# A hybrid decoder step on one core: the first tile's norm in column halves, and its gain spread by GpSimd

## The reference

```python
def layer(x, p, ...):
    mix, pool_buf, v = mixer(rmsnorm(x, norm_mix), ...)   # the first norm; its gain is norm_mix
    x = x + mix
    x = x + moe(rmsnorm(x, norm_ffn), ...)                # top 4 of 32 experts, clamped SwiGLU
    x = x + sigmoid(x @ w_ple_gate) * (p @ w_ple_proj)
    return x, pool_buf, v

def rmsnorm(x, g):
    y = x * lax.rsqrt(jnp.mean(x * x, axis=-1, keepdims=True) + RMS_EPS)
    return y * g

def mixer(h, ...):
    z = h @ w_in          # columns: pooling part z, then u and v of the gating part
    ...                   # pooling mixer and gating mixer, concatenated, @ w_out
```

## Time and profile before

| | us |
|---|---|
| median of 3 runs | 1396.92 |
| lowest and highest | 1396.46, 1397.35 |
| the profiled execution, own time | 1394.86 |
| its span, first to last instruction | 1393.1 |
| PE busy | 1358.1 (97% of the span) |
| DVE busy | 1264.1 (91%) |
| ACT busy | 936.1 (67%) |
| POOL busy | 237.9 (17%) |

### The profile page before, as it was taken

How to read it: one execution, slowest core, us unless ns; L and a number is a source line. 1 busy time by engine, 2 the same in 40 slices (tenths; PEclk the granted TensorE clock), 3 DMA queues, 4 the chain that set the end, 5 groups by cost and what they waited for, 6 DMA issues and landing times.

```text
span 1393.1 us, 19627 instructions
## 1 busy us (share of the span) xinstructions
PE 1358.1 (97%) x6479; PEld 1122.8 (81%) x6479; DVE 1264.1 (91%) x1003; ACT 936.1 (67%) x635; POOL 237.9 (17%) x190
## 2 busy tenths in 40 slices
PE   6999989999999999999999999999999999999997
PEld 5998767888888888888888888888888888888565
DVE  5876578999999999999999999999999999999885
ACT  4313256777777777777777777777777777777532
POOL 3130021112111111111111111111111111110100
PEclk9999979999999999999999999999999999999999
DMA  7112377999999999999999999999999999999551
GB/s 269 61 64 104 143 291 285 383 357 372 391 388 380 385 381 384 381 379 377 379 383 382 379 379 382 381 381 388 384 382 379 384 386 384 380 385 367 192 231 62
DMA packets 94204, 457.09 MB, mean 328 GB/s; under 512 B 13347, under 2 KB 14927, under 8 KB 60310
## 3 DMA queue, kind: packets, MB, share of 16 engines
q1 hardware_dynamic: 84383, 437.77, 80.8%
q0 software_dynamic: 9360, 17.85, 3.3%
q10 hardware_dynamic: 430, 1.08, 0.3%
HBM read 451.50 MB, written 21.58 MB: 340 GB/s over the span
## 4 chain that ended last, share of the span: by engine, by line
PE 95%; DVE 2%; issue 1%; ACT 1%; DMA 1%; POOL 0%; POOLq 0%; DVEq 0%; ACTq 0%
PE ps L1454 50%; PE ps L1463 25%; PE ps L1293 4%; PE ps L1433 2%; PE ps L1440 2%; PE ps L1606 2%; PE ps L1394 1%; PE ps L1202 1%; PE ps L1204 1%; PE ps L1209 1%; PE ps L1149 1%; PE ps L1326 1%; DVE resid L2144 1%; PE ps L1143 1%; PE ps L1146 1%
## 5 line engine op out<-in xcount | busy, mean ns | idle before, releaser
L1923 DVE TENSOR_TENSOR w_lo<-raw,w_hi 128x2048 fp32r<-128x2048 f32 x384 | 870.4, 2298 | 21.5 <-PE ps L1463 21.1
L978 ACT ACTIVATE w_hi<-raw 128x2048 fp32r<-128x2048 f32 x384 | 732.8, 1917 | 229.6 <-PE ps L1454 142.8
L1454 PE MATMUL ps<-w_hi,xT_hi 128*128 128x512 f32 x1024 | 280.0, 395 | 4.5 <-ACT w_hi L978 3.4
L1454 PE MATMUL ps<-w_hi,xT_lo 128*128 128x512 f32 x1024 | 275.8, 391 | 0.0
L1463 PE MATMUL ps<-w_lo,xT_hi 128*128 128x512 f32 x1024 | 274.0, 389 | 0.0
L1454 PEld LDWEIGHTS ps<-w_hi,xT_lo 128*128 128x128 f32 x1024 | 193.6, 189 | 41.1
L1454 PEld LDWEIGHTS ps<-w_hi,xT_hi 128*128 128x128 f32 x1024 | 190.9, 189 | 43.9 <-issue 3.4
L1463 PEld LDWEIGHTS ps<-w_lo,xT_hi 128*128 128x128 f32 x1024 | 192.1, 188 | 40.2 <-DVE w_lo L1923 0.2
L803 POOL PARTITION_BROADCAST up_bias<-bias_rows x32 | 41.5, 1296 | 655.4 <-DVE glu L2003 649.2
L1454 PE MATMUL ps<-w_hi,aT_hi 128*128 128x512 f32 x512 | 140.1, 395 | 0.6 <-ACT aT_hi L997 0.6
L1454 PE MATMUL ps<-w_hi,aT_lo 128*128 128x512 f32 x512 | 137.2, 390 | 0.1
(11 more groups left out here) (297 smaller groups left out, 1218.0 us busy)
## 6 DMA issues: line engine op xcount, KB each, us to landing
raw<-in_w_up_dram SPq DMA_DIRECT2D x256, 1024.0 KB, 7.6
raw<-in_w_down_dram SPq DMA_DIRECT2D x128, 1024.0 KB, 8.0
raw<-in_w_ple_gate_dram SPq DMA_DIRECT2D x4, 1024.0 KB, 4.9
yk<-expert_rows SPq DMA_DIRECT2D x4, 1024.0 KB, 7.7
raw<-expert_rows SPq DMA_DIRECT2D x4, 1024.0 KB, 6.5
resid<-in_x_prompt_dram SPq DMA_DIRECT2D x4, 512.0 KB, 7.7
w_v_sb<-in_w_in_dram SPq DMA_DIRECT2D x2, 1024.0 KB, 8.1
w_z_sb<-in_w_in_dram SPq DMA_DIRECT2D x2, 1024.0 KB, 13.0
```

Of the source, the lines that this page charges most:

```text
L978: act.activation(w_hi[:, s % SPLIT, :], raw[:, slot(s), :], ACT.Copy).then_inc(s_hi, 1)
L1454: mm = pe.matmul(out[:, c:c + 512], (xh, xl)[xs], w_hi[:, s % SPLIT, base + c:base + c + 512], start=(fresh and xs == 0 and base == 0), st ...
L1923: dve.tensor_tensor(w_lo[:, s % SPLIT, :], raw[:, slot(s), :], w_hi[:, s % SPLIT, :].bitcast(F32), ALU.subtract).then_inc(s_lo, 1)
```

## The change

The 4 KB row of `norm_mix` is loaded alone, into the first partition of `x_rows` (a tile that is free until the expert loop), and POOL spreads it over the partitions of `gain` with `partition_broadcast`, after the identity and ahead of the first root. DVE waits for that instead of for the load. For tile 0, the product with root and gain, the transposes, the high part and the low part are each cut in two halves of 512 columns (four blocks), and DVE makes `w_v_low(0)` between the two low halves. `project_v(0, 0)` needs the first halves alone. The counts on `s_job`, `s_xn`, `s_xh` and `s_emptied["V"]` go up by one accordingly. Tiles 1 to 4 are done as before.

```diff
-            EMPTIED[name] = sum(w == who for _, w in JOBS[:n + 1])
+            EMPTIED[name] = sum(w == who for _, w in JOBS[:n + 1]) + (who == "V")
...
             pool.affine_select(out=ident[:], in_=ident[:], compare_op=ALU.not_equal, fill=1.0, base=0,
                                pattern=[[-1, P]], channel_multiplier=1).then_inc(s_ident, 1)
+            pool.wait_ge(ld["gain"], 16)
+            pool.partition_broadcast(gain[:], x_rows[0:1, :]).then_inc(s_gain, 1)
...
-            act.dma_start(gain[:], norm_mix[0].partition_broadcast(P)).then_inc(ld["gain"], 16)
+            act.dma_start(x_rows[0:1, :], norm_mix[0:1, :]).then_inc(ld["gain"], 16)
...
             square1(0)
             w_v_high(0)
-            x_high(0)
+            for half in range(2):
+                act.wait_ge(s_job, 1 + half)
+                act.activation(xTh[:, w_z_halves[half], 0:P], bank(("xT", 0), half).rearrange("p (b n) -> p b n", n=P),
+                               ACT.Copy).then_inc(s_xh, 1)
             square1(1)
...
-                pe.wait_ge(s_xh, t + 1)
+                pe.wait_ge(s_xh, 1 if t == 0 and i == 0 else t + 2)
...
-                    pe.wait_ge(s_emptied["V"], EMPTIED[("xT", t)])
+                    pe.wait_ge(s_emptied["V"], 1 if t == 0 and i == 0 else EMPTIED[("xT", t)])
...
                 if what == "xT":
-                    pe.wait_ge(s_xn, t + 1)
+                    if t == 0:
+                        for k in range(KD):
+                            if k % (KD // 2) == 0:
+                                pe.wait_ge(s_xn, 1 + k // (KD // 2))
+                            mm = pe.transpose(bank(("xT", 0), k // 4)[:, (k % 4) * P:(k % 4 + 1) * P],
+                                              xn[:, 0, k * P:(k + 1) * P], ident[:])
+                            if k % (KD // 2) == KD // 2 - 1:
+                                mm.then_inc(s_job, 1)
+                        project_v(0, 0)
+                        continue
+                    pe.wait_ge(s_xn, t + 2)
                     transposes(("xT", t), xn[:, t % 2, :])
-                    if t == 0:
-                        project_v(0, 0)
...
-            dve.wait_ge(ld["gain"], 16)
+            dve.wait_ge(s_gain, 1)
...
-                dve.scalar_tensor_tensor(out=xn[:, t % 2, :], in0=resid[:, t, :], scalar=rstd1[:, t:t + 1], in1=gain[:],
-                                         op0=ALU.mult, op1=ALU.mult).then_inc(s_xn, 1)
+                for cols in (slice(0, D // 2), slice(D // 2, D)) if t == 0 else (slice(0, D),):
+                    dve.scalar_tensor_tensor(out=xn[:, t % 2, cols], in0=resid[:, t, cols], scalar=rstd1[:, t:t + 1],
+                                             in1=gain[:, cols], op0=ALU.mult, op1=ALU.mult).then_inc(s_xn, 1)
...
             norm1(0)
-            w_v_low(0)
-            x_low(0)
+            for half in range(2):
+                dve.wait_ge(s_xh, half + 1)
+                ks = w_z_halves[half]
+                dve.tensor_tensor(xTl[:, ks, 0:P], bank(("xT", 0), half).rearrange("p (b n) -> p b n", n=P),
+                                  xTh[:, ks, 0:P].bitcast(F32), ALU.subtract).then_inc(s_emptied["V"], 1)
+                if half == 0:
+                    w_v_low(0)
             norm1(1)
```

More of the change, by code:

```diff
@@ L365, in job_filled @@
         def job_filled(eng, name):
-            eng.wait_ge(s_job, JOB[name] + 1)
+            eng.wait_ge(s_job, JOB[name] + 2)
         ld = {n: sem("ld_" + n) for n in (
@@ L397, in build @@
         s_olow = sem("last_tile_low_rows")
+        s_gain = sem("first_norm_weights_spread")
         s_bias_hi = sem("down_bias_hi")
@@ L560, in _ @@
             sp.dma_start(new_pool_sample[0, :, 0:PB - DS, :], state_pool[0, :, DS:PB, :]).then_inc(s_pout, 16)
-            sp.wait_ge(s_job, JOB[("v", LAST)] + 1)
+            sp.wait_ge(s_job, JOB[("v", LAST)] + 2)
             for k in range(0, KD, 4):
@@ L565, in _ @@
             w_out_v = w_out.rearrange("a (i k p) n -> p (a i) k n", p=P, k=KD // 2)
-            sp.wait_ge(s_job, JOB[("z", G - 1)] + 1)
+            sp.wait_ge(s_job, JOB[("z", G - 1)] + 2)
             load(w_out_a[:], w_out_v[:, 0], "w_out")
-            sp.wait_ge(s_job, JOB[("u", G - 1)] + 1)
+            sp.wait_ge(s_job, JOB[("u", G - 1)] + 2)
             load(w_out_b[:, 0:KD // 4, :], w_out_v[:, 1, 0:KD // 4, :], "w_out2")
@@ L625, in _ @@
                     load_bias(0, 0)
-                sp.wait_ge(s_xn, TT + t + 1)
+                sp.wait_ge(s_xn, TT + t + 2)
                 sp.dma_start(xn_dram[t * P:t * P + NT[t], :], xn2[0:NT[t], :]).then_inc(s_xrow[t], 16)
@@ L754, in _ @@
                     src = dst
-            pool.wait_ge(s_job, JOB[("u", G - 1)] + 1)
+            pool.wait_ge(s_job, JOB[("u", G - 1)] + 2)
             pool.memset(x_rows[:], 0.0).then_inc(s_xzero, 1)
@@ L1669, in norm1 @@
                     job_filled(dve, ("xT", t - 2))
-                dve.scalar_tensor_tensor(out=xn[:, t % 2, :], in0=resid[:, t, :], scalar=rstd1[:, t:t + 1], in1=gain[:],
-                                         op0=ALU.mult, op1=ALU.mult).then_inc(s_xn, 1)
+                for cols in (slice(0, D // 2), slice(D // 2, D)) if t == 0 else (slice(0, D),):
+                    dve.scalar_tensor_tensor(out=xn[:, t % 2, cols], in0=resid[:, t, cols], scalar=rstd1[:, t:t + 1],
+                                             in1=gain[:, cols], op0=ALU.mult, op1=ALU.mult).then_inc(s_xn, 1)
             def x_low(t):
-                dve.wait_ge(s_xh, t + 1)
+                dve.wait_ge(s_xh, t + 2)
                 cols = slice(t * P, t * P + NT[t])
```

## The result

The changed kernel takes **1409.48 us** (median of 4 runs, 1408.77 to 1410.38), the kernel before 1396.69 us in the same comparison (median of 4, 1395.58 to 1397.35). The ratio is 1.0098, 95% interval 1.0085 to 1.011: slower by 12.8 us. The forecast was 1408.8 us. The profiled execution of the changed kernel took 1408.80 us, that of before 1394.86 us.

The account below looks back on a forecast made before the run. PE was taken to bound the kernel once it has data, after the first root. Root end 21.1 with two loads, less 8.13 before and 1.1 for halves, gives +11.9 on 1396.92: 1408.8 us, range 1401 to 1415.

Parts of the forecast that it names:

- a shift passes through: From tile 2's transposes on, PE follows PE, so a shift there was claimed to reach the end in full.
- Both pairs paid: POOL's head: configuration pairs ahead of broadcast and first root each cost a code load, 8.2 us each; chance 0.77 within bounds.
- Rival (a): POOL's head: only the first load is paid, root's code returns for nothing; +4.0, 1400.9 us; chance 0.13.
- Rival (b): POOL's head: neither pair costs visible time, halves and smaller load are won; 1394.3 us, not slower; chance 0.04.
- The price of a load: Time from a POOL configuration pair to its operation in the head: 8.2 us, between 6.13 and 10.3.
- the high bound: Dearest load price in the head, 6.13 stretched by the gathers' 7.4 / 4.4: 10.3 us, giving +16.1.
- the middle: Load price of 8.2 us taken between low and high, as gathers queue on DMA engines and no load packets were seen.
- "agree": Claim that the expert loop's 6.13 us from pair to broadcast matches the Trainium skill's 5.95 us for a first call.
- The halves: Tile 0 cut in halves, counted from the first root's end to tile 2's transposes: saves about 1.1 us (1.0 to 1.7).
- The smaller load: 512 KB less head traffic: tile 0 and w_v up to 1.5 us sooner, but nothing gained with the late root.
- The sum: First root's end at 21.1 against 8.13, less 1.1 for the halves: +11.9 us, added to the median 1396.92.
- rest of the load: Possible remainder of a load in a broadcast, from the loop's 3.39 instead of 1.30: 2.1 us more, +18.2 at the high price.

Follow-up runs that it names:

- e1_halves: Changed kernel with the first norm's weights loaded as 512 KB as before, so tile 0's halves alone: 1396.14 us against 1395.62 before, ratio 0.9999.
- e5_pe_spread: Changed kernel with the row spread by two PE matmuls and DVE copies instead of POOL's broadcast: 1394.36 us against 1395.92 before, ratio 0.9988.
- e4_no_root: Changed kernel with the first norm's roots taken off POOL, DVE making a reciprocal of the variance instead, square root left out: 1401.19 us (one run).
- e3_quiet: Changed kernel with SP issuing nothing behind tile 0 until the first root is done, keeping head traffic away: 1408.14 us (one run).
- e2_spread: Kernel before with the small load and POOL's broadcast, tile 0 done whole without halves: 1411.47 us, ratio 1.0111.
- e6_twice: Changed kernel with the broadcast of the gain done twice, no configuration pair between: 1409.29 us (one run).

## Why the prediction was right, and where it was off

**What bounds the kernel, and that a shift passes through.** Right. Tile 2's transposes moved by 13.70 us (21.98 to 35.68), and the profiled executions differ by 13.94. The first gathered rows, at +13.76, and PE's end, at +13.95, show the same shift: the kernels run in step from the head on. For small gains the assumption holds less well: in the profiled executions e1_halves keeps 0.48 of its 0.73 and e5_pe_spread about 0.9 of its 2.76 through the loop. The term that is missing is the stretch of lower clock in the router and the first expert, which need not move with the work.

**Both pairs paid.** Right, and it decided the size; the sign would have been the same with one. The trace of the changed kernel has both idle stretches; e4_no_root, which takes the root off POOL, gets about 8 us back, keeps the first and is still 5.6 over the kernel before. Rival (a), with the code back for nothing, would have had the root at 12 to 13; it started at 22.63. Rival (b) would have had it at 6 to 8. The 0.1 us at L688, which spoke for (a), was no measure of a pair that has code to bring back.

**The price of a load.** The term that was mis-sized is the first: 8.2 taken, 10.55 measured, and 9.95 to 10.33 in the other runs with the full head, so about the high bound of 10.3 or just past it. The step that failed was the choice of the middle: it held that a load might not queue with the other transfers. e3_quiet shows that this load is stretched by the head's traffic from 5.59 to 10.55. The second pair came out at 8.13 against 8.2, but not for the reason given. It was taken to be as dear as the first and stretched alike; it costs 7.3 by itself, and with the engines full 7.26, 7.35, 8.13 and 9.09 in four kernels, so the traffic's share of it lies between nothing and 1.8. By the Trainium skill's figure for both pairs the estimate had been 1404.3; the chip was 5.2 us above it. The prediction's "agree" was too quick: the Trainium skill's 5.95 ("GPSIMD Engine Reference", section 2.1 Instruction dispatch) is the gap less the wait for events, and of the 6.13 in the loop 3.08 was the wait for the gathered rows (184.0 to 187.08). Counted in that way 3.05 would be left. The near figure is the quiet head's 5.59, where the row is there early (at 2.93 in e5_pe_spread) and hardly any of the gap is wait; so the load ran during the wait, as the prediction had read it.

**The halves.** 1.1 taken off; the root's end to tile 2 went from 13.85 to 12.46, which is 1.39, and 1.53 against e2_spread. It lies in the range of 1.0 to 1.7. As foreseen, the transposes ran without a gap and DVE's order set tile 2. What the prediction didn't say is that the number holds only behind a late root. e1_halves shows it: with the root in its old place the split of w_v on ACT is later than the transposes, and the gain is 0.73 at tile 2. Rival (b) took the 1.1 in full for just that case. Its 2.6 us for halves and smaller load together is near the 2.76 that e5_pe_spread, which has both and no broadcast, shows at tile 2, but that is luck: the halves gave less there and the smaller load more.

**The smaller load.** Right that it gives nothing here. Its worth was put too low: tile 0 is squared from 4.10 instead of 5.96, 1.86 sooner, and w_v comes 2.02 sooner (7.01 against 9.03 in the trace of before), where up to 1.5 was taken.

**The sum.** The root ends at 23.22 where 21.1 was forecast; with the halves 0.3 better, the profiled execution shows +13.9 and the medians +12.8, where +11.9 was forecast. The 2.06 added to come from the profiled execution to the median came in at 0.68, since the changed kernel's own profiled execution lies only that much under its median: this took back more than half of what the load was undersized. So a part of the closeness of 1408.8 to 1409.48 is luck. On the profiled executions alone the forecast was 1406.8 and the time 1408.80.

**Open.** Whether a "rest of the load" of 2.1 exists was left at the upper end of the range; e6_twice shows none in the head, and none in its loop either, although the loop's load is paid. The 3.39 of the earlier trace rows is thus no fixed part of a load; what makes it isn't known.

## What to carry to other kernels

Before a GpSimd operation that brings configuration pairs is put beside ordinary ones, find the pairs in the built order, one in and one back, and ask of each who stands behind it on that engine: here they were 10.6 and 8.1 us on the path to save a load of 512 KB whose absence lets tile 0 and the weights land about 2 us sooner. A price read from a quiet stretch can be far too low for a busy one, and each pair has to be asked by itself: the way in went from 5.59 to about 10, the way back by at most 1.8 (7.34 quiet, 7.26 to 9.09 busy). Where one row must reach all partitions at the head, two matmuls with a row of ones on an idle PE did it without any load, and a gain worked out "from the root on" has to be asked once more what else isn't ready when the root is early.

## What the runs showed of the hardware

- The time from the configuration pair to the broadcast grew with the DMA traffic: 5.59 us at a share of 0.14, 6.13 at 0.29, 6.59 at 0.39, and 9.95 to 10.55 at about 1.03. It runs while POOL waits for something else: 3.08 of the 6.13 were such a wait. No row shows what goes on in it; POOL is idle with "issue" as the reason.
- The way back has a price of its own, and another one: 7.34 us with no transfer under way, and 7.26 to 9.09 with the engines full. Kernels at the same share (1.05 and 1.06) differed by 1.8 us: the pairs at 14.2 and 14.5 took 9.09 and 8.13, those at 15.3 and 18.2 took 7.26 and 7.35. What makes that difference is open.
- An affine select ran behind the broadcast without a pair between them (16.11 in e4_no_root); only the iota behind it brought one. So not every change of operation brings a pair; which ones do is read from the built order.
- Spreading a row of 1024 values over 128 partitions took PE 3.75 us (two matmuls, shown as four), from 2.93, in time that it had idle, and DVE two copies of 0.68 us. No configuration pair came with it.
- The lower level of the granted clock did not move with the work: 16 router matmuls took 3.60 us at 0.50 in e5_pe_spread and 2.70 at 0.69 in the kernel before, and a lead of 2.40 us shrank to 0.76 in the first expert.
